# Forgetting attention with scores and outputs in two passes each, two banks for turned probabilities, and low keys copied in ten transfers

## The reference

```python
s = einsum('bhqd,bhkd->bhqk', q, k) * Dh**-0.5      # Dh = 64
s = s + c[t] - c[s]                                 # c = cumsum(log_sigmoid(fz + b_f))
s = where(k_pos <= q_pos, s, -inf)
p = softmax(s);  o = einsum('bhqk,bhkd->bhqd', p, v)
```

## Time and profile before

| | us |
|---|---|
| median of three runs | 1181.19 (1180.79 to 1182.04) |
| the profiled execution's own time | 1180.96 |
| its span in the profile | 1179.2 |
| PE busy | 1158.5 (98%) |
| ACT, DVE, POOL busy | 451.7, 356.3, 489.9 |

### The profile page before, as it was taken

The page is one execution under the profiler, slowest core; times in us unless marked ns, Lnnn a source line. Parts: engine busy times, 40 slices in busy tenths (PEclk is TensorE's granted clock), DMA queues, the critical chain, the costliest instruction groups (busy, mean ns, idle before and its releaser), DMA issues.

```text
span 1179.2 us, 15228 instructions
## 1 busy us (share of the span) xinstructions
PE 1158.5 (98%) x5664; PEld 965.3 (82%) x5664; DVE 356.3 (30%) x718; ACT 451.7 (38%) x740; POOL 489.9 (42%) x223
## 2 busy tenths in 40 slices
PE   9999999999999999999999999999999999999998
PEld 7888888888888778787778988878888888888886
DVE  2221221320005274655554204744131131130003
ACT  6232232331215456455625534545433232232113
POOL 5344354354442633222314853425435435434441
PEclk9999999999999999999999999999999999999999
DMA  6332323323232222111213442213332323222233
GB/s 201 97 101 90 106 89 102 93 92 104 89 108 72 72 90 90 41 55 49 89 55 110 158 161 90 84 49 120 101 95 92 104 89 106 89 96 101 90 107 108
DMA packets 84989, 113.03 MB, mean 96 GB/s; under 512 B 8846, under 2 KB 53964, under 8 KB 84940
## 3 DMA queue, kind: packets, MB, share of 16 engines
q1 hardware_dynamic: 84848, 112.34, 29.5%
q10 hardware_dynamic: 92, 0.02, 0.0%
HBM read 110.24 MB, written 2.10 MB: 95 GB/s over the span
## 4 chain that ended last, share of the span: by engine, by line
PE 61%; issue 25%; POOL 11%; DVE 2%; DMA 0%; ACT 0%; POOLq 0%; SPq 0%; DVEq 0%
PE bank L1426 20%; PE bank L1427 20%; PE bank L1430 20%; POOL w_lo L578 10%; PE bank L1467 1%; DVE h L1063 1%; DMA raw<-in_ffn_w_gu 0%; POOL q_lo L616 0%; POOL q_hi L616 0%; DVE tmp L1052 0%; DVE bank L1052 0%; PE bank L1503 0%; ACT xh L648 0%; PE bank L1488 0%; PE bank L1445 0%
## 5 line engine op out<-in xcount | busy, mean ns | idle before, releaser
L578 POOL TENSOR_TENSOR w_lo<-raw,w_hi 128x1024 fp32r<-128x1024 f32 x200 | 478.8, 2404 | 666.8 <-ACT w_hi L634 666.0
L1426 PE MATMUL bank<-xh,w_hi 128*128 128x512 f32 (+1 forms) x912 | 349.7, 383 | 1.2 <-POOL w_lo L578 1.1
L1427 PE MATMUL bank<-xh,w_lo 128*128 128x512 f32 (+1 forms) x912 | 348.4, 382 | 0.0
L1430 PE MATMUL bank<-xl,w_hi 128*128 128x512 f32 (+1 forms) x912 | 348.3, 382 | 0.0
L634 ACT ACTIVATE w_hi<-raw 128x1024 fp32r<-128x1024 f32 x200 | 209.0, 1057 | 350.2 <-DMA raw<-in_ffn_w_down 167.5
L1426 PEld LDWEIGHTS bank<-xh,w_hi 128*128 128x128 f32 x912 | 171.5, 188 | 34.9 <-POOL w_lo L578 1.5
L1430 PEld LDWEIGHTS bank<-xl,w_hi 128*128 128x128 f32 x912 | 171.4, 188 | 33.2
L1427 PEld LDWEIGHTS bank<-xh,w_lo 128*128 128x128 f32 x912 | 171.6, 188 | 31.9
L1426 PE MATMUL bank<-w_hi,mid_hi 128*128 128x512 f32 x352 | 137.3, 390 | 0.0
L1427 PE MATMUL bank<-w_hi,mid_lo 128*128 128x512 f32 x352 | 137.0, 389 | 0.0
L1430 PE MATMUL bank<-w_lo,mid_hi 128*128 128x512 f32 x352 | 137.0, 389 | 0.0
(11 more groups left out here) (232 smaller groups left out, 1216.4 us busy)
## 6 DMA issues: line engine op xcount, KB each, us to landing
raw<-in_ffn_w_gu SPq DMA_DIRECT2D x176, 256.0 KB, 2.9
raw<-in_ffn_w_down SPq DMA_DIRECT2D x88, 256.0 KB, 2.8
raw<-in_mix_w_in SPq DMA_DIRECT2D x48, 256.0 KB, 2.8
raw<-in_mem_w_kv SPq DMA_DIRECT2D x32, 256.0 KB, 3.1
raw<-in_mem_w_o SPq DMA_DIRECT2D x24, 256.0 KB, 2.9
raw<-in_mix_w_out SPq DMA_DIRECT2D x16, 256.0 KB, 3.0
raw<-in_mem_w_q SPq DMA_DIRECT2D x16, 256.0 KB, 2.8
h<-in_x SPq DMA_DIRECT2D x4, 512.0 KB, 5.4
```

Of the source, the lines that this page charges most:

```text
L578: gp.tensor_tensor(w_lo[:, n % SLOTS, :], raw[:, n % SLOTS, :], w_hi[:, n % SLOTS, :].bitcast(F32), ALU.subtract).then_inc(lo_ready, 1)
L1426: pe.matmul(dst, w[0], x[0], start=start, stop=False, skip_group_check=loose)
L1427: pe.matmul(dst, w[1], x[0], start=False, stop=False, skip_group_check=loose)
L1430: return pe.matmul(dst, w[0], x[1], start=False, stop=stop, skip_group_check=loose)
```

## The change

Each head's pairs are laid out so that one pass over the array's 128 rows does the work of two.

- Scores. `q_hl` holds in 64 partitions the high part of a head's q and in the other 64 its low part. `k_hi` and the low keys (`k_lo_a`, `k_lo_b`, `k_lo_c`) hold a head's keys twice, once in each half. So q_hl by k_hi gives high by high plus low by high, and q_hl by key_lo gives high by low plus low by low. Two products in place of three.
- Outputs. `v_hl` holds the high and the low part of a head's v side by side as 128 columns. Two products (by `pt_hi` and by `pt_lo`) give 64 rows of each; the two halves of bank 3 are added afterwards: ACT copies one half to `fox_y`, DVE adds the other to it (semaphore `y_sum`), and one turn later ACT rounds the sum (`round_rows`) and DVE subtracts (`low_rows`).
- The second copies of the keys are made by ten DMA transfers on ACT's queue, between the halves of SBUF: four for `k_hi`, two for `k_lo_a`, two each for `k_lo_b` and `k_lo_c`. PE waits for the first half's copies before the attention loop, and for the second half's before head 4. POOL's four memsets go.
- Banks. Turned probabilities use banks 1 and 2 in turn; scores use bank 0 alone, so the scores of unit k wait for the maximum of unit k-1. The decay row of the next head is multiplied into bank 3 in turn 4 hd + 1 and no longer in turn 4 hd + 3.
- The first extraction of keys by ACT and DVE goes by halves of 64 partitions: 8 instructions in place of 4 on each.

```diff
+        q_hl = sb("q_hl", [P, FOX_H, SEQ], F32R, at=shared)
+        k_hi = sb("k_hi", [P, FOX_H, SEQ], F32R, at=shared + 16 * kib)
+        v_hl = sb("v_hl", [P, TC, FOX_H, P], F32R, at=shared + 32 * kib)
...
+        def fp_bank(k):
+            return bank[1 + k % 2]
+        def cum_bank(hd):
+            return bank[3 if hd else 0]
...
-                    gp.memset(heads[:, :, e, :].bitcast(F32), 0.0).then_inc(q_zero, 1)
...
+                        for e, done in enumerate((k_even_hi, in_hi)):
+                            r = head_rows(e)
+                            act.activation(k_hi[r, 2 * m + e, :], tmp[r, m, :], ACT.Copy).then_inc(done, 1)
+                        if m % 2:
...
+                                act.dma_start(heads[head_rows(e + 1), :, :].bitcast(F32),
+                                              heads[head_rows(e), :, :].bitcast(F32)).then_inc(k_hi_twin[m // 2], 16)
...
+            def low_twins(half):
+                act.wait_ge(k_even_lo, 2 * half + 2)
+                act.wait_ge(in_lo, 6 + 6 * half)
+                for t in ((k_lo_b, k_lo_c) if half else (k_lo_a,)):
+                    heads = t[:, :, :].rearrange("p (j e) n -> p j e n", e=2)
+                    for e in range(2):
+                        act.dma_start(heads[head_rows(e + 1), :, e, :].bitcast(F32),
+                                      heads[head_rows(e), :, e, :].bitcast(F32)).then_inc(k_lo_twin[half], 16)
...
+                def low_rows(done):
...
                     dve.wait_ge(y_h, hd + 1)
-                    dve.tensor_tensor(fox_lo[r, c, :], bank[3][r, :], fox_hi[r, c, :].bitcast(F32),
+                    dve.tensor_tensor(fox_lo[r, c, :], fox_y[r, c, :], fox_hi[r, c, :].bitcast(F32),
                                       ALU.subtract).then_inc(y_l, 1)
...
-                    fox_free(fox_slot(k))
+                    if k:
+                        pe.wait_ge(maxed, k)
...
-                    three(dst, (q_hi[:, hd, tok], q_lo[:, hd, tok]), (key_hi(c)[:, 0:w], k_lo[:, c, 0:w]),
-                          False, True, True).then_inc(scored, 1)
+                    pe.matmul(dst, q_hl[:, hd, tok], k_hi[:, hd, 0:w], start=False, stop=False, skip_group_check=True)
+                    pe.matmul(dst, q_hl[:, hd, tok], key_lo(hd)[:, 0:w], start=False, stop=True,
+                              skip_group_check=True).then_inc(scored, 1)
...
-                    if k:
-                        pe.wait_ge(pt_l, k)
+                    if k >= 2:
+                        pe.wait_ge(pt_l, k - 1)
...
+                        for pt in (pt_hi, pt_lo):
+                            last = pe.matmul(bank[3][:, q0:SEQ], v_hl[:, j, hd, :], pt[:, j, q0:SEQ],
...
+                pe.wait_ge(k_hi_twin[0], 16 * 2)
+                pe.wait_ge(k_lo_twin[0], 16 * 2)
                 fox_attention()
```

More of the change, by code:

```diff
@@ L349, in build @@
         in_tmp = sem("in_tmp")
-        q_zero = sem("q_zero")
+        k_even_hi = sem("k_even_hi")
+        k_even_lo = sem("k_even_lo")
+        k_hi_twin = [sem(f"k_hi_twin{i}") for i in range(2)]
+        k_lo_twin = [sem(f"k_lo_twin{i}") for i in range(2)]
         q_even_hi = sem("q_even_hi")
@@ L820, in cum_spread @@
                     act.wait_ge(maxed, TC * (hd - 1))
-                act.activation(cum_b[:, hd % 2, :], bank[cum_slot(hd) % 2][:, :], ACT.Copy).then_inc(cb_ready, 1)
+                act.activation(cum_b[:, hd % 2, :], cum_bank(hd)[:, :], ACT.Copy).then_inc(cb_ready, 1)
             def fox_attention():
@@ L830, in output, with round_rows @@
                     act.wait_ge(pv_done, hd + 1)
-                    r = slice(FOX_D * (hd % 2), FOX_D * (hd % 2 + 1))
-                    act.activation(fox_hi[r, hd // 2, :], bank[3][r, :], ACT.Copy).then_inc(y_h, 1)
+                    r, other = fox_rows_of(hd), fox_rows_of(hd + 1)
+                    act.activation(fox_y[r, hd // 2, :], bank[3][other, :], ACT.Copy).then_inc(y_part, 1)
+                def round_rows(done):
+                    if not 0 <= done < N_FOX or FOX_UNITS[done][1] < TC - 1:
+                        return
+                    hd = FOX_UNITS[done][0]
+                    r = fox_rows_of(hd)
+                    act.wait_ge(y_sum, hd + 1)
+                    act.activation(fox_hi[r, hd // 2, :], fox_y[r, hd // 2, :], ACT.Copy).then_inc(y_h, 1)
                 for k in range(N_FOX + LATE + 2):
-                    if k < N_FOX - 1 and k % TC == TC - 1:
-                        cum_spread(k // TC + 1)
+                    if k == 4:
+                        low_twins(1)
                     if k < N_FOX:
@@ L1154, in fox_attention @@
                             dve.wait_ge(pturned, k - PROBS + 1)
[L1155 removed]
+                        dve.tensor_tensor_reduce(prob[:, k % PROBS, 0:w], bank[0][:, 0:w],
                                                  cum_b[:, hd % 2, 0:w], -1.0, -NEG, ALU.add, ALU.min,
@@ L1666, in cum_rows @@
             def cum_rows(hd):
-                pe.matmul(bank[cum_slot(hd) % 2][:, :], sel[:, hd:hd + 1].to_broadcast([P, P]), cum_hl[:, :],
+                pe.matmul(cum_bank(hd)[:, :], sel[:, hd:hd + 1].to_broadcast([P, P]), cum_hl[:, :],
                           start=True, stop=True).then_inc(cb_done, 1)
             def fox_attention():
[L1673 to L1678, removed]
                 def scores(k):
@@ L1713, in output @@
                     if hd:
-                        pe.wait_ge(y_l, hd)
+                        pe.wait_ge(y_sum, hd)
                     else:
                         pe.wait_ge(pt_zero, 2)
+                    if hd + 2 < FOX_H:
+                        pe.wait_ge(cb_ready, hd + 3)
                     for j in range(TC):
[L1718 to L1721, removed]
+                        q0 = min(j, 2) * P
+                        for pt in (pt_hi, pt_lo):
+                            last = pe.matmul(bank[3][:, q0:SEQ], v_hl[:, j, hd, :], pt[:, j, q0:SEQ],
+                                             start=j == 0 and pt is pt_hi, stop=j == TC - 1 and pt is pt_lo,
+                                             skip_group_check=True)
                     last.then_inc(pv_done, 1)
@@ L1726, in fox_attention @@
                         scores(k)
+                    if k % TC == 1 and k // TC + 1 < FOX_H:
+                        if k // TC >= 2:
+                            pe.wait_ge(y_sum, k // TC - 1)
+                        cum_rows(k // TC + 1)
                     fill(k)
```

113 lines of the change are left out of this document (64 added, 49 removed).

## The result

| | before | changed |
|---|---|---|
| median, us (5 runs each) | 1180.98 (1180.61 to 1182.04) | 1201.32 (1200.74 to 1203.84) |
| ratio to before | | 1.0173 (95%: 1.0161 to 1.0184) |
| span of the profiled execution | 1179.2 | 1199.3 |
| mean granted clock of PE | 0.999 | 0.992 |

The account below looks back on a forecast made before the run. PE was taken as the bound, busy 1158.5 of 1179.2 us. Terms -10.3 + 5.7 - 1.0 + 9.9 + 6.3 + 1.5 - 5.0 + 0.7 = +7.8 on 1180.96 gave a forecast median of 1189.0 us, range 1177.5 to 1195.5.

Parts of the forecast that it names:

- blocked low halves, four: Turns 7, 15, 23, 27: PE waits while POOL's split holds up DVE's low half; 9.9 us more (0 to 12.4).
- heads 2 and 3, GLA's work: Turns 10 to 13: DVE's group 3 extractions and first GLA products stand before a maximum; 6.3 us more.
- small waits: Six other units of the loop: short waits for the maximum, 0.1 to 0.7 us each; 1.5 more (0 to 4).
- waits for low probabilities gone: Loop's transposes: a second bank for turned probabilities ends five listed waits and small ones; 5.0 us less (3.1 to 6).
- The passes: Scores and outputs in the loop: one pass in three goes, 1.28 us a head, 10.3 us less for eight.
- The maximum is late: Loop: scores wait for the previous unit's maximum, queued on DVE; new waits of 9.9, 6.3 and 1.5, 17.7 us.
- PE starts 5.7 us late: Loop's head: PE waits for the key copies, landing at 458.1; 5.7 us late (4.2 to 7.6).
- Its waits give 1.0 back: Loop's start: the values' low parts, which hold the first two maxima, finish during the pause; 1.0 us less.
- I price it at 2.5 and leave it out of the sum: First turns after the pause: PE's clock may fall to half rate; 2.5 us (0 to 4), not summed.
- POOL's memsets at 0: POOL's memsets go from a stretch where PE waits for nothing: no gain, 0 us.
- More than forecast: Rival, 1192 to 1195 us: copies land at 460 or the clock falls, +1.9, +2.5 or both; chance 0.14.
- Faster: Rival, about 1176 us: removed passes count and maxima come in time, new waits below 7.5 us; chance 0.17.

Follow-up runs that it names:

- e8: e7 with a third pass put back in each score and each output; 1187.47 us.
- e2: Changed kernel with the low keys' copies issued earlier, ahead of the decay work, and the second half's keys copied inside the loop; 1190.38 us.
- e1: Changed kernel with eight full fp32 dummy products keeping PE busy in the pause ahead of the loop; 1199.24 us.
- e4: Changed kernel with the low half of a head's output moved two turns later on DVE; 1189.31 us.
- e5: Changed kernel with ACT rounding each weight block of the loop one turn later, so POOL's splits move too; 1204.36 us.
- e3: Changed kernel with the banks as before: two for scores and decay rows, one for turned probabilities; 1195.32 us.
- e7: Changed kernel with early copies of low keys and low halves two turns later, banks as changed; 1179.59 us.
- e6: Changed kernel with early copies of low keys, low halves two turns later and the banks of the kernel before; 1178.80 us.

## Why the prediction was wrong

The account of the 20.1 us, forecast and measured:

| term | forecast | measured | from |
|---|---|---|---|
| third passes | -10.3 | -10.1 | e8 |
| blocked low halves, four | +9.9 | +9.8 | waits of 1.69, 2.67, 2.65, 2.77 |
| heads 2 and 3, GLA's work | +6.3 | +5.8 | waits of 1.45, 1.71, 2.68 |
| small waits | +1.5 | +1.6 | 0.39, 0.96, 0.25 |
| restart after a wait, not listed | 0 | +1.8 | 10 x 0.18, an estimate |
| waits for low probabilities gone | -5.0 | -4.0 | the 3.1 of the earlier trace rows and 5 x 0.18 |
| given back after the pause | -1.0 | 0 | e2 |
| start of the loop | +5.7 | +8.7 | first mask |
| clock after the pause | 0 | +2.8 | e1 |
| clock within the loop | 0 | +3.2 | two turns, 1.6 each |
| behind the loop | +0.7 | +0.8 | |
| sum | +7.8 | +20.4 | of 20.1 |

The terms come to 0.3 us more than the measured 20.1.

- **The passes: right.** 1.26 a head where nothing is waited for.
- **The maximum is late: right**, in turns and size, and in what is blocked. Four blocked low halves in the turns named (only that turn 23 waited in full too), one long wait behind a GLA product, 17.2 us listed against 17.7. e4 takes the low half away and 9.4 go; e5 moves the splits and the median low half falls from 1.35 to 0.69 us. Only the part of the single score bank was overrated, as e3 shows. The Trainium skill (SBUF — State Buffer, "Who interferes with whom") names the cause, an exclusive lock between a VectorE operation with two inputs in SBUF and a GpSimd one that reads SBUF; the trace agrees: 0.7 us alone, 2.0 when it begins 0.9 after a split's start.
- **"PE starts 5.7 us late": the first step that failed**, by how long the copies take. From the first issue to the last landing I had 4.7 us (453.4 to 458.1). It was 8.9 (451.86 to about 460.8). Both prices in it were too low. An issue was priced at 0.3 from one transfer of 4 KB at the start, and the four took 0.6, 0.6, 0.6 and 1.6 us. The landing was priced from the rate of transfers over all partitions; the last two took 6.7 and 6.9 from their issue. In e2, where the other pair went out 2.6 us before them and not 1.4, the same two took 3.4 and 4.0, so nearly half of the 6.8 comes from what else was under way then, of which the other pair stands nearest. No run parts the causes. My upper bound, 460.0, was near the truth only because ACT began its issues 1.5 us earlier than I had it. The Trainium skill (SBUF — State Buffer, "Door 1: The DMA port swizzle") gives 64 partitions about half of the rate. By its 5.3 us for the megabyte and 1.2 fixed, the four would take 6.5 us, as an estimate, and the two in e2 3.9. Measured are 8.9 and 4.6: slower than the full rate, as the Trainium skill has it, but its figure alone does not give the landing, and no run compares 64 partitions with 128.
- **"Its waits give 1.0 back": wrong.** The values' low parts do hold the first maximum, and e2 shows it: 0.9 us that the pause hides. But the sum had no wait there from which it could be given back.
- **"I price it at 2.5 and leave it out of the sum": the second step that failed.** The clock did fall, and e1 has the price: 2.8. It was a rival with a chance of 0.14 and belonged in the sum: a pause of several us was forecast, and the only row on PE after it had done nothing, at the span's start, showed half the rate. The Trainium skill (TensorE: Matmul & The Clock Gate, Part 1) has the clock fall after idleness too, and the trace agrees: a granted clock of 0.82 from 452.3 to 480. That waits of 2.7 us within the loop can also bring it was in no part of the prediction; it is 3.2 us more.
- **"POOL's memsets at 0": wrong by 1.1, in the kernel's favour.** The list of PE's waits of the kernel before has one that I had not taken in, which ends at 394.39 us:

```profile
PE bank L1426 <- POOL w_lo L578: 1.1, 1, 1.1
```

Here POOL's memsets, from 384.50 to 391.88, delay a split. The changed kernel has no wait there, and its work at 405 to 440 is 1.1 earlier (the first key copy at 439.58, 440.64 in the earlier trace rows). This is in the 8.7 already; so is a new wait of 0.7 for a weight block at 446.56, because ACT rounds it after four halves and two issues. No run moves the memsets alone, so these two are read from the traces only.
- **The rivals.** "More than forecast" held, beyond its own 1192 to 1195, since both its additions came and a third beside them. "Faster" fell: the new waits are 17.2 and not under 7.5. e7 and e6 come near it, at 1179.6 and 1178.8, once the pause and about half of these waits are taken away.

The range ended at 1195.5. It held both additions of that rival, at 1.9 and 2.5 us; they came to 3.0 and 2.8. It held nothing for the drops within the loop (3.2), the restarts (1.8) and the 1.0 that was not given back.

## What to carry to other kernels

A change that shortens PE's work per step has to be read at the other engines' chain from result to result: here 10.1 us less work on PE met 17.2 us of new waits, over half of them because one operation of 0.7 us stood ahead of PE's next input and could be blocked for 2. Put late work (the low half, which nobody needs for two turns) behind the operation for which PE waits; one place in the order was worth 12.0 us. A transfer on the path is to be issued when its input is ready and not where the code is convenient (10.9 us), and a forecast pause of PE gets the price of its clock in the sum, once for each long pause.

## What the runs showed of the hardware

- A transfer from one half of SBUF to the other (64 partitions, 256 KB) cost ACT's queue 0.6 to 0.7 us to issue, and 1.6 as the fourth in a row. In e2 two of them landed 3.4 and 4.0 us after their issue; four in a row in the changed kernel landed after 3.8, 5.4, 6.7 and 6.9.
- A subtraction of 64x512 with both inputs in SBUF took DVE 0.7 us, and 2.0 when it began inside a POOL operation of 2.4 us: it ended 0.55 after that one. A product of 128x1024 took 1.22 and 2.64.
- After a pause of 8.7 us PE ran its first products at half rate, 2.8 us lost. In e1's trace eight full fp32 products in the pause avoid it.
- A wait of 2.6 to 2.8 us was followed in some places by a drop of the clock to 1.2 GHz that cost 1.6 us, and in others, with the same wait, it wasn't. What decides between them stays open.
